# HGRN2 and NSA decoder step on one core: nine gate tiles of each layer split by GpSimd, the sample outputs of HGRN2 in two parts, final squares added on GpSimd

## What is computed

```python
def token_mixer(h, pos, past, w_in, ...):
    hq, hf, hi, hg, nq, kc, vc, ks, vs, kw, vw, ngate, mgate = jnp.split(h @ w_in, splits, axis=-1)
    o_hg, s_hg = hgrn2_mixer(hq, hf, hi, hg, lb, hg_norm, s0)      # gated linear attention, 4 heads of 128
    ...                                                            # compressed, selected and window attention
    o_nsa = g[:, :, 0] * o_cmp + g[:, :, 1] * o_slc + g[:, :, 2] * o_win
    branches = jnp.einsum('blnc,ncd->blnd', jnp.stack([o_hg, o_nsa], axis=2), w_branch)
    mg = jax.nn.sigmoid(mgate).reshape(B, L, N_BRANCH, D_MODEL)
    return jnp.sum(mg * branches, axis=2) @ w_out, ...

def hgrn2_mixer(q_raw, f_raw, i_raw, g_raw, lb, norm_g, s0):
    ...
    o, s_final = gla_chunked(q, k, v, log_f, s0, chunk)            # samples: one chunk each, from state s0
    o = rmsnorm(o, norm_g) * silu(g_raw)                           # g_raw is hg

# per layer: x += token_mixer(rmsnorm(x)); x += conv_ffn(rmsnorm(x)); at the end y = rmsnorm(x, norm_final)
```

## Time and profile before

| what | value |
|---|---|
| median of 3 runs | 1156.46 us (1153.97 to 1159.42) |
| profiled execution, its time | 1153.79 us |
| its span, first to last instruction | 1152.0 us |
| PE busy | 1125.9 us, 98% |
| DVE, ACT, POOL busy | 710.1, 545.8, 192.8 us |
| mean granted TensorE clock | 0.985 |

### The profile page before, as it was taken

The page is one execution under the profiler, slowest core; times in us unless marked ns, Lnnn a source line. Parts: engine busy times, 40 slices in busy tenths (PEclk is TensorE's granted clock), DMA queues, the critical chain, the costliest instruction groups (busy, mean ns, idle before and its releaser), DMA issues.

```text
span 1152.0 us, 20868 instructions
## 1 busy us (share of the span) xinstructions
PE 1125.9 (98%) x8473; PEld 1023.6 (89%) x8473; DVE 710.1 (62%) x1305; ACT 545.8 (47%) x867; POOL 192.8 (17%) x318
## 2 busy tenths in 40 slices
PE   6999999999999999999999999999999999999997
PEld 5988766778999999999999787776899999999997
DVE  5798165557567777763578835545656677777343
ACT  4543365553356555542444335655434555555232
POOL 2156300012121000100024560000312101100000
PEclk8999999989999999999999999999899999999998
DMA  9556331347644444344456535223684444432411
GB/s 295 160 156 217 110 95 52 111 120 219 220 147 146 147 147 148 114 141 163 146 124 208 184 97 158 74 68 114 177 266 152 149 153 155 155 124 92 168 41 46
DMA packets 151749, 165.90 MB, mean 144 GB/s; under 512 B 31596, under 2 KB 114406, under 8 KB 151398
## 3 DMA queue, kind: packets, MB, share of 16 engines
q1 hardware_dynamic: 151654, 164.58, 45.6%
HBM read 156.16 MB, written 12.46 MB: 146 GB/s over the span
## 4 chain that ended last, share of the span: by engine, by line
PE 92%; DVE 3%; DMA 2%; ACT 1%; issue 1%; SPq 1%; DVEq 0%; ACTq 0%
PE mm L696 65%; PE ax L696 23%; PE ax L699 3%; DMA ring<-in_state_hgrn 1%; ACT mixb L1329 1%; DVE ring_low L1693 1%; DMA ring<-in_state_conv 1%; ACT work_parts L1329 0%; SPq L498 0%; DVE mixb L1848 0%; DVE mixb L2127 0%; DVE work_parts L2096 0%; PE mm L699 0%; DVE cstT L1755 0%; DVE mixb L1865 0%
## 5 line engine op out<-in xcount | busy, mean ns | idle before, releaser
L696 PE MATMUL mm<-work_parts 128*128 128x320 f32 (+1 forms) x1088 | 345.7, 318 | 6.4 <-DVE h_low L1687 4.1
L1693 DVE TENSOR_TENSOR ring_low<-ring,work_parts 128x2048 fp32r<-128x2048 f32 (+2 forms) x116 | 256.0, 2207 | 128.3 <-ACT work_parts L1329 127.9
L696 PE MATMUL mm<-h_low,work_parts 128*128 128x320 f32 x1024 | 321.0, 313 | 0.0
L696 PE MATMUL mm<-work_parts,ring_low 128*128 128x320 f32 x1024 | 317.2, 310 | 0.0
L1329 ACT ACTIVATE work_parts<-ring 128x2048 fp32r<-128x2048 f32 (+2 forms) x116 | 212.2, 1829 | 152.6 <-PE mm L696 82.4
L696 PEld LDWEIGHTS mm<-work_parts 128*128 128x128 f32 x1088 | 206.5, 190 | 13.0 <-issue 7.0
L696 PEld LDWEIGHTS mm<-h_low,work_parts 128*128 128x128 f32 x1024 | 194.5, 190 | 0.3
L696 PEld LDWEIGHTS mm<-work_parts,ring_low 128*128 128x128 f32 x1024 | 194.6, 190 | 0.0
L696 PE MATMUL ax<-act_parts,work_parts 128*128 128x320 f32 x544 | 126.1, 310 | 0.6 <-DVE ring L2118 0.6
L696 PE MATMUL mm<-act_parts,work_parts 128*128 128x320 f32 x480 | 117.2, 309 | 0.0
L696 PE MATMUL mm<-hT,ring 128*128 128x320 f32 x384 | 109.6, 437 | 0.0
(11 more groups left out here) (247 smaller groups left out, 1589.5 us busy)
## 6 DMA issues: line engine op xcount, KB each, us to landing
ring<-in_w_gate_up SPq DMA_DIRECT2D x44, 1024.0 KB, 7.0
ring<-in_w_in SPq DMA_DIRECT2D x10, 2048.0 KB, 7.9
ring<-in_w_in SPq DMA_DIRECT2D x18, 1024.0 KB, 5.9
ring<-in_w_down SPq DMA_DIRECT2D x8, 1536.0 KB, 6.7
ring<-in_w_out SPq DMA_DIRECT2D x4, 2048.0 KB, 13.2
ring<-in_w_down SPq DMA_DIRECT2D x4, 2048.0 KB, 7.9
ring<-in_w_in SPq DMA_DIRECT2D x32, 128.0 KB, 3.5
ring<-in_cache_cmp_kv SPq DMA_DIRECT2D x32, 128.0 KB
```

The source lines that it names most:

```text
L696: return nc.tensor.matmul(out, lhsT, rhs, start=start, stop=stop)
L1693: V.tensor_tensor(unit_of(u, ring_r), unit_of(u, ring), unit_high(u).bitcast(F32), ALU.subtract).then_inc(*st.up(w_low[l]))
```

## The change

Per layer nine of the twelve plain tiles become split tiles: `hg3`, `mga0` to `mga3`, `mgb0` to `mgb3` (`GATE_TILES`). GpSimd makes their parts. It copies the 8 tiles of `hT` to `n_high` (over keys and factors no longer used), subtracts them in place once the plain tile `hg2` is full (`h_low`), and takes the weights by halves of 4 products (128x512): a copy to one of three buffers `half_high`, then a subtraction in place. Half n may be copied when half n - 3 has been used. The copies of `h` and the low part on ACT and DVE go away, and `n_high` serves the later gate tiles m = 4 to 7 too. Some buffers move (`oX`, `vX`, the compressed sums).

`sample_outputs` is cut by heads: heads 0 and 1 (`st0`), the tile `mga4`, heads 2 and 3 (`st1`), the tile `mgb4`. ACT and DVE split unit MGU + 1 right behind MGU + 0. The second `values_by_sequence` waits for `op1`.

At the end GpSimd adds the squares of tiles 0 to 6 one onto the next, and PE sums two tiles instead of eight.

```diff
+GATE_TILES = ["hg3"] + [f"mg{y}{m}" for m in range(4) for y in "ab"]
-        oX = [part(mixb, at, 512)... for at in (1280, 1792, 3840, 4352)]
+        oX = [part(work, 5376 + 512 * n, 512)... for n in range(4)]
+        n_high = [part(act_r, at + T * n, T) for at in (1280, 3840) for n in range(4)]
+        half_high = [part(*at, 512)... for at in ((act_r, 6640), (act_r, 7152), (work_r, 6280))]
...
+            def gate_tile(name, first=0, end=KD):
+                n = GATE_TILES.index(name)
+                bank = MM[L].bank(name) if first else begin(MM[L], name)
+                for k in range(first, end):
+                    half, kk = 2 * n + k // 4, k % 4
+                    if kk == 0 or k == first:
+                        pe.wait_ge(half_low, 2 * len(GATE_TILES) * L + half + 1)
+                    if n == 0:
+                        pe.wait_ge(n_lo, KD * L + k + 1)
+                    last = split_products(bank[:, 0:T], half_high[half % 3][:, kk, :], gate_half(half, ring_r)[:, kk, :],
+                                          n_high[k], h_low[:, k, :], k == 0, k == KD - 1)
+                    if k == 3:
+                        last.then_inc(half_used, 1)
...
-                out_gate(3, l)
+                gate_tile("hg3")
                 turned(1)
-                merge_gate(0, 0, l)
+                gate_tile("mga0")
...
                 prompt_outputs()
-                sample_outputs(l)
-                pe.wait_ge(h_lo[L], 1)
-                split_gates(4)
+                sample_outputs(0, l)
+                split_gate(4, 0)
+                sample_outputs(1, l)
+                split_gate(4, 1)
...
                         if final and k == NJ - 1 and l == DEPTH - 1:
+                            if m == 0:
+                                turned_back(0, (0, 1, 2, 3), (0, 1))
                             if m == 1:
-                                turned_back(0, (0, 1, 2, 3))
-                                end_sums((0, 1, 2, 3))
+                                turned_back(0, (0, 1, 2, 3), (2,))
                             if m == 2:
-                                end_sums((4, 5))
                                 turned_back(1, (4, 5))
                             if m == 3:
-                                end_sums((6,))
                                 turned_back(1, (6,))
-            end_sums((KD - 1,))
+            pe.wait_ge(end_added, 1)
+            end_sums(KD - 2)
+            pe.wait_ge(end_sq, KD)
+            end_sums(KD - 1)
...
-                A(h_high, hT, ACT.Copy).then_inc(*st.up(h_hi[L]))
                 split(MGU + 0, l)
+                split(MGU + 1, l)
...
-                low(h_low, hT, h_high, h_lo[L])
                 split(MGU + 0, l)
+                split(MGU + 1, l)
...
+                def high_of_gates(n):
+                    b = GATE_TILES[n // 2]
+                    po.wait_ge(*landed_at("w_hg" if b[0] == "h" else f"mg{int(b[3]) // 2}", l))
+                    if n < 3:
+                        if n == 2:
+                            po.wait_ge(rows_ready[L], NSEQ + 1)
+                            po.wait_ge(kv_stored[L], 16 * 6)
+                    elif n % 2:
+                        po.wait_ge(half_used, len(GATE_TILES) * L + (n - 3) // 2 + 1)
+                    else:
+                        po.wait_ge(*MM[L].filled(GATE_TILES[(n - 3) // 2]))
+                    link(G.tensor_copy(half_high[n % 3], gate_half(n, ring)))
+                def low_of_gates(n):
+                    G.tensor_tensor(gate_half(n, ring_r), gate_half(n, ring), half_high[n % 3].bitcast(F32),
+                                    ALU.subtract).then_inc(*st.up(half_low))
                 values_by_sequence(0)
+                po.wait_ge(h_ready[L], KD)
+                for k in range(KD):
+                    last = G.tensor_copy(n_high[k], hT[:, k, :])
+                link(last)
+                po.wait_ge(*AXR[L].filled("krt3"))
+                for n in range(3):
+                    high_of_gates(n)
+                    low_of_gates(n)
+                po.wait_ge(*MM[L].filled("hg2"))
+                for k in range(KD):
+                    G.tensor_tensor(h_low[:, k, :], hT[:, k, :], n_high[k].bitcast(F32), ALU.subtract).then_inc(
+                        *st.up(n_lo))
+                for n in range(3, 2 * len(GATE_TILES)):
+                    high_of_gates(n)
+                    low_of_gates(n)
+                po.wait_ge(*AXR[L].filled("op1"))
                 values_by_sequence(1)
...
+            for m in range(1, KD - 1):
+                po.wait_ge(end_sq, m + 1)
+                last = G.tensor_tensor(sq[:, m, :], sq[:, m - 1, :], sq[:, m, :], ALU.add)
+                last.then_inc(*st.up(pool_step))
+                po.wait_ge(*st.settled())
+            po.sem_inc(end_added, 1)
```

105 lines of the change are left out of this document (51 added, 54 removed).

## The result

The changed kernel takes 1149.9 us (median of 10 runs, 1147.1 to 1152.9) against 1156.9 us for the kernel before (10 runs): a ratio of 0.995, with a 95% interval from 0.993 to 0.997. It is 7 us faster, not 25, and the time lies outside the predicted range. The profiled execution has a span of 1145.4 us, 6.6 less than before.

The account below looks back on a forecast made before the run. PE, busy for 98% of the span, was taken as the bound: A 9.0, B 11.8 and C 4.5 make 25.3 us off the profiled 1153.8, plus 2.7 for the median: 1131 us, range 1123 to 1142.

Parts of the forecast that it names:

- A: Nine gate tiles per layer split, parts made by GpSimd: 4.5 us saved a layer, 9 in all.
- The saving of a tile: Each gate tile, once split, saves PE 0.98 us (4.50 to 3.52); nine save 8.8 us a layer.
- Lost cover: Shorter tiles hide less of the softmaxes in attention, so PE waits come back: 1.3 us a layer.
- Contention: GpSimd slows DVE at six places of attention, 0.5 us each: 3 us a layer lost.
- B: Sample outputs in two parts, no copies of `h`: PE's wait for `st1` goes, clock stays full, 11.8 us saved.
- No wait for the parts: In attention GpSimd makes the gate tiles' parts in time, a half in about 2.2 us; PE never waits for them.
- The first: Rival: in attention each of six places waits for a whole GpSimd subtraction, 1142 us; chance 0.17, shared with zero tile gain otherwise.
- The fourth: Rival: GpSimd becomes the bound of attention, slower if a half takes over 5.3 us; 1178 us at 6; chance 0.05.
- The fifth: Rival: softmax latency, not PE's work, sets attention, so splitting tiles gains zero; 1140 us; within a shared chance of 0.17.
- second rival: Clock stays at 1.2 GHz behind the gates, from sample outputs' small products; their split gives 3.8 us, 1139; chance 0.08.
- C: At the end, GpSimd adds the squares of tiles 0 to 6: 4.5 us saved, between 3.4 and 4.6.
- The test named beforehand: Forecast is wrong if attention isn't at least 2 us a layer shorter, or PE waits at `mga4` or `br`.

Follow-up runs that it names:

- `hg3` plain: The changed kernel with `hg3` a plain tile again and the low parts of `h` made by DVE behind it: 1146.7 us, ratio 0.993.
- `hg3` plain, new dealing: The changed kernel with `hg3` plain, `h`'s low parts on DVE, merge-gate products dealt 3, 10, 7, 4 and 10, 7, 5, 2: 1141.9 us.
- plain tiles: The changed kernel with its nine tiles as plain float32 products again, while GpSimd does all its work: 1160.8 us, ratio 1.002.
- new dealing alone: The changed kernel with only the merge-gate products dealt out anew between sample steps (3, 10, 7, 4 and 10, 7, 5, 2): 1147.8 us.

## Why the prediction was wrong, step by step

For A the sum of a layer was -8.8 (tiles) + 1.3 (cover) + 3.0 (contention) = -4.5 us. Layer 0 gave -6.2 + 0.9 + 4.8, and 4.4 us of slow clock for which the sum had no term: +3.9. So of 8.4 us of error the clock is 4.4, the saving of the tiles 2.6 and contention 1.8, less 0.4 of cover. The steps that failed are these three, the clock above all.

**The saving of a tile** was taken as 0.98 us, from four split tiles in a row. The pieces as they stand, among other steps, save 6.2 us and not 8.8 (the sum over the eleven pieces of layer 0 from start to next start at full clock, 40.0 before and 33.8 after). The chain of the kernel before had a row for a split tile by itself:

```profile
264.10 3.73 PE mm L696 x24
```

That is 3.73 and not 3.52. Nine of those save 6.9, which was there to be read.

**Lost cover** was 1.3 us a layer; with GpSimd idle it is 0.9. Right in size.

**Contention** was 3.0; it is 4.8 us of waits in layer 0: 1.5 at the second prompt softmax (1.95 against 0.47 with the low parts elsewhere) and 3.3 at the samples (4.3 less 0.9). What failed in this term is "each meets a busy GpSimd less than half of the time". It treats a softmax as one instruction. It is a chain of nine small ones in a row, several of which meet a subtraction, and each that does pays for the rest of it. The counter-argument "most of the DVE work there reads PSUM" doesn't hold for this chain: all nine (L2088 to L2095) read and write SBUF. The places were right, but for the last prompt unit, where GpSimd happened to be idle.

**The clock** is the term that was missing: 4.4 us in layer 0 (1.75 for the 20 products right behind the wait of 1.95 us, 4.41 from start to next start and not 2.66; 1.3 for `hg3`; 1.3 for the seven products behind the wait of 1.43). The prediction used just this effect in B, from the earlier trace rows, and did not ask whether the waits that it allowed in A would do the same. That step is over half of the error. Most of it follows from contention: with GpSimd idle behind `hg3` the clock is 1.00 behind the sample softmaxes, and with `hg3` plain as well no wait of attention has a slow stretch behind it.

**No wait for the parts** held: no wait names POOL, a half takes 0.61 + 1.28 us and a gap, 2.0 against 2.2 forecast, and the low parts of `h` took 7.58 us against 7.2. But the prediction only asked whether they come in time, not beside what they run; they start at 157.23, on top of the second softmax.

**The rivals.** The first (contention takes all of A, 1142) had the mechanism and was still too mild, since its price was one subtraction at a place and no clock. Its chance of 0.17 was too low: the rule that the prediction itself cites for it was at hand, the rows that agree with it too, and the middle of the range was taken between ends that were far apart. The fourth, GpSimd as the bound, did not come. The fifth said that A is zero because softmax latency sets attention; with GpSimd idle attention gets 2.9 us shorter (105.3 to 102.4, 4.4 without the slow stretch at `hg1`), so it doesn't.

**B** gave 10.5 us of 11.8. The wait went and the clock stayed at 1.00, so the second rival is out. Missing are mainly the two tiles at 3.73 and not 3.52 (0.8 us in both layers). **C** gave 4.0 of 4.5; GpSimd's last addition ran under the down projection, as forecast. B and C do without A: 1147.3 us with an extra wait of 1.72 us a layer that A's copies on GpSimd would remove.

The test named beforehand (wrong if attention isn't shorter by 2 us a layer) decided it: it was 3.7 and 3.8 us longer.

## What to carry to other kernels

Work moved to an idle GpSimd isn't free where DVE runs a chain of short SBUF instructions with PE behind it: price each of these instructions with the rest of the GpSimd instruction that it can meet, keep GpSimd's instructions short, and put them where DVE reads PSUM or rests. When work between two waits gets shorter, deal it out again so that the longest softmax has the most of it over it, and look what the new dealing sets free on the other engines. A wait on PE costs more than its length if the clock falls behind it. Which waits do that can't be read off their length here (next section), so give an estimate with and without it; in the kernels with split tiles only waits from 1.10 us on had a slow stretch behind them.

## What the runs showed of the hardware

DVE's instructions on PSUM were not held up: the copy of 128x512 from PSUM (L1895) takes 0.68 us at 160.74, in the middle of GpSimd's 7.58 us of subtractions, as in the kernel before (L1872 at 158.91, both shown above). SBUF instructions of 2 to 64 columns beside a subtraction took up to 1.34 us. It goes the other way too: a copy on GpSimd that starts behind DVE's scaling of 2048 columns takes 2.36 us instead of 0.61, and both end within 0.5 us.

```profile
173.80 2.29 DVE L1888 TENSOR_TENSOR attb<-attb,wt 128x2048 f32<-128x2048 f32 x1
```

```profile
174.20 2.36 POOL L2420 CAST work_parts<-ring 128x512 fp32r<-128x512 f32 x1 [0.91 <-PE mm L707]
```

In attention PE fell to 1.2 GHz behind each wait of 1.95 us (six kernels, both layers), and in both layers behind waits of 1.79, 1.75, 1.14 and 1.10 us and 1.43 us in the changed kernel. At the same place of the same kernel it fell in one layer and not in the other behind waits of 1.68 and 1.69 us and 1.64 and 1.61 us (`hg3` plain), 1.42 us (`hg3` plain, new dealing), and 1.26 and 0.88 us (plain tiles). It didn't fall behind 1.69 and 1.70 us in the changed kernel (seven products at 232.29 took 3.33), 1.28 and 1.29 us with the new dealing, nor behind the longest of all, 1.98 us in layer 1 of the new dealing alone. The shortest wait with a fall behind it is in layer 1 of the kernel with plain tiles, where seven products then take 5.22 us from start to next start and not 3.86:

```profile
770.87 1.14 PE L710 MATMUL ax<-consts,attb 128*128 128x128 f32 x6 [0.88 <-DVE attb L2094]
...
772.02 5.29 PE L707 MATMUL mm<-h_low,ring_low 128*128 128x320 f32 x14
```

The longest without one, where the same six transposes take 0.87 us:

```profile
772.53 0.87 PE L710 MATMUL ax<-consts,work 128*128 128x128 f32 x6 [1.98 <-DVE work L2095]
```

And in four layers of three kernels it fell at `hg1` with no wait before it. So the length of a wait doesn't settle it; what else decides stays open.
